# Turning the query columns of the second mixing stage by DMA, with two smaller edits of the same stage

## The reference

```python
q = rmsnorm_2(q, q_g)
k = rmsnorm_2(k, k_g)
logits = jnp.einsum('bqhcd,bkhcd->bhcqk', q_blk, k).astype(jnp.float32) * scale
logits = logits + bias[None, :, None]
logits = jnp.where(rel >= 0, logits, -jnp.inf)
p = jax.nn.softmax(logits, axis=-1)
attn = p[:, :, 0] - lam * p[:, :, 1]
out = jnp.einsum('bhqk,bkhe->bqhe', attn, v)
out = rmsnorm_2(out, subln_g) * (1.0 - lambda_init)
```

## Time and profile before

| | |
|---|---|
| median of 3 runs | 998.8 us (998.78 to 998.86) |
| the profiled execution's own time | 998.68 us |
| its span, first to last instruction | 996.9 us |
| TensorE / VectorE / ScalarE / GpSimd busy | 99% / 69% / 55% / 12% |
| granted TensorE clock over the span | 1.000 |
| second mixing stage | from 565.5 us to 749.5 us |

### The profile page before, as it was taken

How to read it: one execution, slowest core, us unless ns; L and a number is a source line. 1 busy time by engine, 2 the same in 40 slices (tenths; PEclk the granted TensorE clock), 3 DMA queues, 4 the chain that set the end, 5 groups by cost and what they waited for, 6 DMA issues and landing times.

```text
span 996.9 us, 12571 instructions
## 1 busy us (share of the span) xinstructions
PE 990.9 (99%) x4626; PEld 813.0 (82%) x4626; DVE 688.2 (69%) x1009; ACT 548.4 (55%) x752; POOL 116.0 (12%) x109
## 2 busy tenths in 40 slices
PE   9999999999999999999999999999999999999998
PEld 7788888888877888888888878888888888888887
DVE  6766566668987667656666677797689767656663
ACT  7444343576765546444343576768885555443541
POOL 0000000022200000000000041168914000000000
PEclk9999999999999999999999999999999999999999
DMA  8987776585443546666656376457555546787761
GB/s 264 291 256 254 236 247 211 194 309 175 144 152 130 170 140 202 227 213 203 224 186 228 125 259 211 148 170 211 149 188 197 205 152 207 232 218 225 231 191 43
DMA packets 158985, 199.87 MB, mean 200 GB/s; under 512 B 49617, under 2 KB 105050, under 8 KB 158810
## 3 DMA queue, kind: packets, MB, share of 16 engines
q1 hardware_dynamic: 158922, 199.24, 62.2%
q10 hardware_dynamic: 16, 0.00, 0.0%
HBM read 182.45 MB, written 5.77 MB: 189 GB/s over the span
## 4 chain that ended last, share of the span: by engine, by line
PE 97%; DMA 2%; ACT 1%; SPq 0%; issue 0%; DVE 0%; ACTq 0%
PE bank L1897 23%; PE bank L1899 23%; PE bank L1898 23%; PE bank L2005 7%; PE bank L2003 7%; PE bank L2004 7%; PE bank L1912 1%; PE bank L2054 1%; DMA raw<-in_w_in 1%; PE bank L2168 1%; DMA raw<-in_ffn_w_gu 0%; PE bank L2069 0%; PE bank L2056 0%; PE bank L2126 0%; PE bank L2289 0%; PE bank L2290 0%
## 5 line engine op out<-in xcount | busy, mean ns | idle before, releaser
L1897 PE MATMUL bank<-hi,xh 128*128 128x512 f32 (+1 forms) x944 | 375.2, 397 | 1.0 <-DVE lo L1515 0.6
L1899 PE MATMUL bank<-hi,xl 128*128 128x512 f32 (+1 forms) x944 | 367.3, 389 | 0.0
L1898 PE MATMUL bank<-lo,xh 128*128 128x512 f32 (+1 forms) x944 | 366.5, 388 | 0.0
L1277 DVE TENSOR_TENSOR lo<-raw,hi 128x2048 fp32r<-128x2048 f32 (+1 forms) x111 | 254.0, 2289 | 146.7 <-ACT hi L799 146.6
L799 ACT ACTIVATE hi<-raw 128x2048 fp32r<-128x2048 f32 (+1 forms) x114 | 216.6, 1902 | 133.4 <-PE bank L2005 96.9
L1897 PEld LDWEIGHTS bank<-hi,xh 128*128 128x128 f32 x944 | 177.3, 188 | 39.7 <-issue 3.3
L1899 PEld LDWEIGHTS bank<-hi,xl 128*128 128x128 f32 x944 | 177.2, 188 | 37.4
L1898 PEld LDWEIGHTS bank<-lo,xh 128*128 128x128 f32 x944 | 177.5, 188 | 34.3
L1294 DVE TENSOR_TENSOR lo<-raw,hi 128x1024 fp32r<-128x1024 f32 (+1 forms) x108 | 133.1, 1243 | 40.7 <-ACT hi L808 40.1
L2003 PE MATMUL bank<-hi,hh 128*128 128x512 f32 x304 | 118.9, 391 | 0.0
L2005 PE MATMUL bank<-hi,hl 128*128 128x512 f32 x304 | 118.4, 389 | 0.0
(11 more groups left out here) (265 smaller groups left out, 963.1 us busy)
## 6 DMA issues: line engine op xcount, KB each, us to landing
raw<-in_w_in SPq DMA_DIRECT2D x48, 1024.0 KB
raw<-in_ffn_w_gu SPq DMA_DIRECT2D x82, 512.0 KB
raw<-in_ffn_w_down SPq DMA_DIRECT2D x22, 1024.0 KB
raw<-in_w_up SPq DMA_DIRECT2D x16, 1024.0 KB
raw<-in_w_down SPq DMA_DIRECT2D x16, 1024.0 KB
raw<-in_w_out SPq DMA_DIRECT2D x8, 1024.0 KB
distance_table<-ftab SPq DMA_DIRECT2D x8, 576.0 KB
raw<-in_w_proj_attn SPq DMA_DIRECT2D x4, 1024.0 KB
```

The lines of the kernel that those rows point to most:

```text
L1277: nc.vector.tensor_tensor(lo[s][:, :, 0:width], raw[s][:, :, 0:width], hi[s][:, :, 0:width].bitcast(F32), ALU.subtract).then_inc(lo_done, 1)
L1897: nc.tensor.matmul(o, sh, wh, start=first and j == 0, stop=False)
L1898: nc.tensor.matmul(o, sh, wl, start=False, stop=False)
L1899: ins = nc.tensor.matmul(o, sl, wh, start=False, stop=last and j == 3)
```

## The change

Three edits in the second mixing stage, and what they need:

- The query columns (c = 0 and 3) are no longer transposed by TensorE. ScalarE makes the planes of 16 bits of a token tile in quarters 4, 5 (c = 0) and 16, 17 (c = 3), at the head of the quarter, behind a wait for `k_qn`. SyncE issues two DMA transposes behind the units of c = 3 and two behind those of c = 6. VectorE merges both token tiles in one instruction in quarter 7 and in quarter 20, behind `head_scale` and ahead of its split of the weights, and counts 2 into `k_trev`. The query gain is no longer applied to the queries: it is multiplied into the gain of the keys once, at the start. TensorE's key groups keep their waits on `k_trev` (`list(M2_T).index(key)`: 2, 3, 6 and 7).
- The reciprocal of the first softmax's sum is applied by ScalarE as a scale of the output's copy, in two instructions for a head in place of one. VectorE multiplies the second softmax's factor by the first's sum, and then makes one scaled addition for each part in place of a scale and a scaled addition.
- The four lambda loads are issued by ScalarE at the head of its quarter 0. SyncE's wait for `n_sq` stands behind the units of c = 2, ahead of the bias load.

```diff
+M2_PLANES = {4: (0, 0), 5: (0, 1), 16: (3, 0), 17: (3, 1)}
+M2_MERGE = {7: 0, 20: 3}
...
+            def flip_queries(c):
+                for t in range(NT):
+                    sp_eng.wait_ge(ffns[1].planes, 2 * (NF1 - 1) + 2 * (c // 3) + t + 1)
+                    sp_eng.dma_start_transpose(q_turned_planes_of(c)[:, :, t * P:(t + 1) * P],
+                                               q_planes_of(c)[:, t, :]).then_inc(ffns[1].flip[t], 16)
...
-                if c == 1:
+                if c in (3, 6):
+                    flip_queries(c - 3)
+                if c == 2:
                     sp_eng.wait_ge(n_sq, 8)
-                    for j, name in enumerate(("lambda_q1_2", "lambda_k1_2", "lambda_q2_2", "lambda_k2_2")):
-                        vector = a[name].rearrange("a n -> (a n)")
-                        sp_eng.dma_start(lamv[:, j, :], vector.partition_broadcast(P)).then_inc(lam_in, 16)
-                if c == 2:
                     sp_eng.dma_start(bias_2[:, :, :], skewed(2 * NH, SEQ)).then_inc(bias_2_in, 16)
...
+                if p == 0:
+                    for j, name in enumerate(("lambda_q1_2", "lambda_k1_2", "lambda_q2_2", "lambda_k2_2")):
+                        vector = a[name].rearrange("a n -> (a n)")
+                        act.dma_start(lamv[:, j, :], vector.partition_broadcast(P)).then_inc(lam_in, 16)
+                if p in M2_PLANES:
+                    cc, tt = M2_PLANES[p]
+                    act.wait_ge(k_qn, 4 * (cc // 3) + tt + 1)
+                    nc.scalar.activation(q_planes_of(cc)[:, tt, :].rearrange("p (s c) -> p s c", s=2),
+                                         hid[:, tt, :].bitcast(U16).rearrange("p (c s) -> p s c", s=2),
+                                         ACT.Copy).then_inc(ffns[1].planes, 1)
...
-                        nc.scalar.activation(xn[:, :, h * P:(h + 1) * P],
-                                             O[h % 2][:, 0:SEQ].rearrange("p (t c) -> p t c", t=NT),
-                                             ACT.Copy).then_inc(k_oev, 1)
+                        for tt, o in ((1, O[h % 2][:, P:SEQ]), (0, O[h % 2][:, 0:P])):
+                            ins = nc.scalar.activation(xn[:, tt, h * P:(h + 1) * P], o, ACT.Copy,
+                                                       scale=inv[:, 4 * h + 1 - tt:4 * h + 2 - tt])
+                        ins.then_inc(k_oev, 1)
...
-                        step(nc.vector.tensor_scalar(c1, c1, lam[:, 4:5], None, ALU.mult))
-                        for q, s in enumerate((slice(0, SEQ), slice(SEQ, SPAN))):
-                            one = l2[:, 1, h % 3, s]
-                            ins = nc.vector.tensor_scalar(one, one, inv[:, 4 * h + 2 + q:4 * h + 3 + q], None, ALU.mult)
-                            ins = ins if q == 0 else step(ins)
+                        step(nc.vector.scalar_tensor_tensor(c1, c1, lam[:, 4:5], sums[:, 4 * h:4 * h + 2],
+                                                            ALU.mult, ALU.mult))
                         for q, s in enumerate((slice(0, SEQ), slice(SEQ, SPAN))):
                             zero = l2[:, 0, h % 3, s]
-                            ins = nc.vector.scalar_tensor_tensor(zero, zero, inv[:, 4 * h + q:4 * h + q + 1],
-                                                                 l2[:, 1, h % 3, s], ALU.mult, ALU.add)
+                            ins = nc.vector.scalar_tensor_tensor(zero, l2[:, 1, h % 3, s],
+                                                                 inv[:, 4 * h + 2 + q:4 * h + 3 + q],
+                                                                 zero, ALU.mult, ALU.add)
...
+                if p in M2_MERGE:
+                    cc = M2_MERGE[p]
+                    for tt in range(NT):
+                        dve.wait_ge(ffns[1].flip[tt], 16 * (NF1 - 1) + 16 * (cc // 3) + 16)
+                    if cc == 3:
+                        dve.wait_ge(k_trev, 4)
+                    dst = q_2[:, 4 * (cc // 3):4 * (cc // 3) + 4, :]
+                    nc.vector.tensor_copy(dst.bitcast(U16).rearrange("p k (c s) -> p s k c", s=2),
+                                          q_turned_planes_of(cc).rearrange("p (s k) c -> p s k c", s=2)
+                                          ).then_inc(k_trev, 2)
...
-                if key is not None and not by_dma(key[0]):
+                if key is not None and key[0] in (1, 4):
                     cc, tt = key
-                    order = list(M2_T).index(key)
-                    if order >= 1:
-                        pe.wait_ge(k_trev, order)
+                    pe.wait_ge(k_trev, list(M2_T).index(key))
                     pe.wait_ge(k_qn, 2 * (0, 1, 3, 4).index(cc) + tt + 1)
```

More of the change, by code:

```diff
@@ L307, in program, with q_planes_of, q_turned_planes_of @@
                 otl = sb("otl", [P, 8, SEQ], F32R, s2)
+        def q_planes_of(c):
+            words = (rg if c == 0 else grt)[:, 0:4, :].rearrange("p b c -> p (b c)")
+            return words.bitcast(U16).rearrange("p (t c) -> p t c", t=NT)
+        def q_turned_planes_of(c):
+            words = (rg if c == 0 else grt)[:, 4:8, :].rearrange("p b c -> p (b c)")
+            return words.bitcast(U16).rearrange("p (k c) -> p k c", c=SEQ)
         lamv = pt2[:, 0, 0:4 * HD].rearrange("p (a b) -> p a b", b=HD)
@@ L1130, in _ @@
                 key = key_at(M2_T, p)
-                if key is not None and not by_dma(key[0]):
+                if key is not None and key[0] in (1, 4):
                     cc, tt = key
-                    order = list(M2_T).index(key)
-                    act.wait_ge(k_tr, order + 1)
+                    if key == (1, 0):
+                        act.wait_ge(cols_done, 5)
+                    act.wait_ge(k_tr, 2 * (cc // 3) + tt + 1)
                     view = X[0][:, :].rearrange("p (k c) -> p k c", c=P)
                     rows = slice(tt * P, (tt + 1) * P)
[L1137 to L1140, removed]
+                    nc.scalar.activation(k_2[:, 4 * (cc // 3):4 * (cc // 3) + 4, rows], view, ACT.Copy,
+                                         scale=cols[:, C_GAIN + 5:C_GAIN + 6]).then_inc(k_trev, 1)
                 for h in range(NH):
@@ L1160, in _ @@
                         m = 2 * (0, 1, 3, 4).index(c) + t
-                        if m >= 2:
-                            act.wait_ge(k_tr, m - 1)
+                        if c == 3:
+                            act.wait_ge(k_tr, t + 1)
+                        if c in (1, 4):
+                            act.wait_ge(ffns[1].planes, 2 * (NF1 - 1) + 2 * (c // 3) + t + 1)
                         nc.scalar.activation(hid[:, t, :], G[t][:, :], ACT.Copy, scale=rstd).then_inc(k_ev, 1)
@@ L1172, in _ @@
                         if c == BY_DMA[0]:
-                            act.wait_ge(k_tr, 7 + t)
+                            act.wait_ge(k_tr, 3 + t)
                         nc.scalar.activation(hid[:, t, :], G[t][:, :], ACT.Copy, scale=rstd).then_inc(k_ev, 1)
@@ L1576, in constants @@
                                             ALU.mult).then_inc(cols_done, 1)
+                dve.wait_ge(cols_done, 4)
+                g = C_GAIN + 4
+                nc.vector.tensor_tensor(cols[:, g + 1:g + 2], cols[:, g:g + 1], cols[:, g + 1:g + 2],
+                                        ALU.mult).then_inc(cols_done, 1)
             ffn(ffns[0], width_of, constants)
```

## The result

| | before | changed |
|---|---|---|
| median, runs side by side | 998.34 us (16 runs) | 1001.81 us (16 runs) |
| lowest and highest | 997.67, 998.92 | 1000.38, 1002.48 |
| the profiled execution | 998.68 us | 1002.13 us |
| its span | 996.9 us | 1000.2 us |
| granted TensorE clock over the span | 1.000 | 0.998 |

The ratio is 1.0031, with a 95% interval of 1.0024 to 1.0038: the change costs 3.5 us, 0.3%. That is within the range (997.2 to 1002.8), but the forecast was "no change" at 1000.2, and by its size the result is the case of "slower by over 0.2%". The 16 runs lie in two groups. Seven have a granted clock of 0.999 or 1.000 and take 1000.38 to 1000.88 us, 2.1 us over before by their median of 1000.45; nine have 0.998 and take 1001.66 to 1002.48, 3.8 us over by their median of 1002.13. The forecast is near the first group (it said +1.4); it has no term for the second.

The account below looks back on a forecast made before the run. TensorE, busy 99% of the span, was taken as the bound. Removed transposes -1.76, wait at quarter 8 -0.59, new waits +1.5 and +2.2 sum to +1.4 us on 998.8: 1000.2 us, range 997.2 to 1002.8.

Parts of the forecast that it names:

- no change: Whole kernel: 1000.2 us, less than the 2.0 us (0.2%) a measurement can tell; chance of same 0.52.
- slower by over 0.2%: Quarter 9, merge in quarter 7: flips land after 8.1 us, wait 3.7 us, sum +3.6, 1002.4 us; chance 0.36.
- Removed transposes: TensorE, c = 0 and 3, two token tiles: four groups of four transposes at 0.44 us go, -1.76 us.
- the wait at quarter 8: TensorE's wait on ScalarE's late `hid` copy of c = 1 goes, -0.59 us.
- Load order at the start: c = 2's first unit issued near 568, planes from 582.0, `hid` copy done 587.7; ScalarE's four issues cost at most 0.3 us.
- First wait: Quarter 9: TensorE's key group waits for quarter 7's merge, itself waiting for flips landing after 5.9 us; +1.5 us.
- the first wait vanishes: Quarter 9: what follows by the skill's rule that transposing DMAs are about as fast as ordinary ones; not summed.
- Second merge: Quarter 21: TensorE's key group waits for quarter 20's merge, behind the last key tile's `head_scale`; +2.2 us.
- The sum: Whole kernel: two savings and two new waits add to +1.4 us, 1000.2 us.
- First flips land in time: Quarter 9: flips land in 2.3 to 4.4 us, no wait there, sum -0.1 us, 998.7; chance 0.12.
- Nobody waits: Quarters 9 and 21: both merges ready, -2.35 us, 996.5, including waits absorbed in an unseen way; chance 0.12.

Follow-up runs that it names:

- lambda_only: Kernel before with only SyncE's four lambda loads issued by ScalarE; 997.86 us, ratio 0.9997.
- no_dma_turn: Kernel before with the lambda-load and reciprocal edits, queries still turned by TensorE; 997.92 us, ratio 0.9996.
- flips_first: Changed kernel with the first two query flips issued ahead of unit U+7 in place of behind it; 999.98 us, ratio 1.0013.
- merge_q19: Changed kernel with the second query merge moved from quarter 20 to quarter 19; 998.38 us, ratio 1.0000.
- own_count_later: Changed kernel with the merges counted on their own semaphore and placed in quarters 8 and 19; 996.39 us, ratio 0.9982.
- second_queries_only: Changed kernel with only the c = 3 queries turned by DMA, c = 0 left to TensorE; 1000.43 us, ratio 1.0019.
- merge_behind: Changed kernel with the c = 3 merge placed behind quarter 20's weight half on VectorE; 1003.52 us, ratio 1.0053.

## Why the prediction was right in its steps and short in its sum

- **Removed transposes, -1.76 us, and the wait at quarter 8, -0.59.** Right. There are 16 matmuls fewer, and the wait is gone; its price comes out as 0.74 us in the rows of `lambda_only` and `no_dma_turn`, 0.15 over the forecast, though their medians can't tell it from nothing. TensorE's arrival at quarter 9 (593.85 + 0.23 = 594.08) is the forecast 594.06, and that is in part luck: it holds the 0.23 us of quarter 6, which the forecast lacked, made good by those 0.15 us and by a stage that starts 0.1 us earlier in this execution (565.37 for 565.47).
- **Load order at the start.** Right: first unit of c = 2 issued at 568.31 (forecast 568), planes at 581.91 (582.0), `hid` copy ended at 586.67 + 0.67 = 587.3 (587.7). The four loads on ScalarE's queue took 0.37 to 0.46 us each from 572.1 on, beside its activations, and no cost of them shows (`lambda_only` is 0.78 us shorter in TensorE's rows).
- **A wait that wasn't foreseen, +0.23 us, quarter 6.** The group (0, 0) behind quarter 5's matmuls had also covered VectorE's low part of the next weights, which ends near 583.0 both before and after. Without its 0.44 us TensorE arrives at 582.84 and stands to 583.07. That the releaser is this low part is argued from the times; the wait is too short for the profile to name one.
- **First wait, 1.5 us forecast, 1.90 measured.** The mechanism is right: the merge stands for the flips, TensorE for the merge, and `flips_first` takes it all away. The size is off because 5.9 us was taken for the landing of the second flip and it was 6.4; the first took 6.8 but was down 0.9 us sooner. The rival named "about 6.5 us on" as deciding, and the second flip landed just short of it. The Trainium skill, "Advanced Engine Details and Errata", section on the X-bar transpose, has transposing DMAs about as fast as ordinary ones. No run here speaks against that: an ordinary load of 512 KB, issued right behind a 1 MB load of this stage, took 6.3 us to landing in the changed kernel,

```profile
wax<-in_w_rg_a SPq DMA_DIRECT2D x1, 512.0 KB, 6.3
```

where a flip moves 256 KB. What did not follow is the prediction's step from the rule to "the first wait vanishes": in this stage ordinary DMAs take as long. It was right to leave that out of the sum.
- **Second merge, 2.2 us forecast, 2.15 measured.** Right, by its own steps: ScalarE idle 2.37 us ahead of the planes of quarter 16, VectorE at the last `head_scale` at 634.49 for 634.0 and TensorE ready at 634.31 for 633.8, both 0.5 us later since the stage lost that much more around the first wait, merge of 1.30 us, and the flips not what is late. Its cause is the order on VectorE: `merge_q19` removes the wait by one place in that order.
- **The sum, the step that failed.** "-1.76 - 0.59 + 1.5 + 2.2 = +1.4 us" adds waits as if TensorE came back from each at the clock with which it went. The missing term is the granted clock behind the second wait, +1.6 us in the profiled execution; 9 of 16 runs show the lower clock, so it is in the median. Without it the miss is 0.7 us (+2.1 for +1.4): 0.4 of the first wait and 0.23 of quarter 6. Nothing in the trace of before showed it, since no wait of TensorE in the stage is listed with more than 0.4 us; the price should have been bounded and the slower case given more than 0.36.
- **The rivals.** "Slower by over 0.2%" came out in its time (1002.4 forecast, 1001.81 measured) and not in its mechanism: of the 2.1 us between the sum of +1.4 and the 3.5 measured only 0.4 is the first wait's. "First flips land in time" is what `flips_first` builds, and it has 998.5 to 999.3 at full clock for the forecast 998.7. "Nobody waits" is what `own_count_later` builds, 996.39 for the forecast 996.5. Both times match better than the differences do, since the forecasts were laid on a median of 998.8 from three runs and before took 998.29 beside these: +0.5 for -0.1, and -1.9 for -2.35. The way to it, "absorbed in a way I don't see", was in the diff: the index in the key group's wait counted merges that the bank no longer needed.

## What to carry to other kernels

When a producer is moved to another engine, go through every wait on its semaphore and ask what each still protects; here a count kept from the old path made TensorE stand 4 us in two places for data that it needed three quarters later. A TensorE-bound kernel can pay for a wait twice, once in the wait and once more when the clock has fallen behind it (here behind waits of 2.14 to 3.28 us, and not behind one of 1.8), so a sum of waits needs a term for the clock and a look at the spread of the runs. If a merged copy waits on a DMA, put it in its engine's order as late as its reader allows, and ahead of the work that follows a late result.

## What was not expected of the hardware

- Of the kernels with a second wait of 2.15 us (2.14 in `second_queries_only` and `flips_first`), 9 of 16, 6 of 11 and 6 of 11 runs show the lower clock, and the others of the same kernel none; with 3.28 us 5 of 5; `merge_q19`, with only the first wait of 1.80 us, in none of 11. The falls end by themselves, with TensorE busy. They cost 1.4 to 1.7 us in the three kernels with the shorter wait (the distance of their groups of runs) and 3.1 in the profiled execution of `merge_behind`. Three executions with the lower clock were profiled, those of the change, `merge_behind` and `flips_first`, and their fall stands behind the second wait; that it stands there in the others is inferred from `merge_q19`. Why one execution falls and the next doesn't is left open. So is whether the first wait never brings a fall because it is shorter or because of where it stands: no kernel has the longer wait in quarter 9.
- The second of two DMA transposes issued back to back keeps SyncE's queue for 4.4 us, where the first takes 1.25. Issued later it keeps it less. In `flips_first` it is issued 2.4 us behind the first, at 585.67, and takes 2.9 us; of the recurrence columns' pairs in the changed kernel, the one issued 2.9 us behind takes 2.0:

```profile
648.49 1.24 SPq L660 DMA_TRANSPOSE act_out<-ig  x1
...
L660 SPq DMA_TRANSPOSE late_t<-ig x1: 2022/2022/2022, 651.4 to 651.4; - x1
```

In every pair of the stage in these two kernels the second flip lands 0.8 to 0.9 us behind the first, whether it was issued 1.3 or 3.5 us behind it (in one pair of before, issued 2.6 us apart, it was 2.3 us). So issuing the two of a pair apart shortens the hold on the queue and not the landing of the pair. That one transpose waits for the other is a guess from this; no run shows it.
